# Two transformer blocks on one core: order of the last residuals, sums of squares and gate products as split matmuls

## The reference

```python
def rmsnorm(x, g):
    return x * rsqrt(mean(x * x, -1) + EPS) * g

def second_block(x, ...):                       # x: output of the first block
    proj = rmsnorm(x, norm1_g) @ w_in
    xa, ya, sq, sk, sv, dq, dk, dv = split(proj)
    xa = causal_dwconv(xa, conv_a_w) + conv_a_b              # 4 taps
    r = sigmoid(einsum('bsnc,ncd->bsnd', xa, w_rgate) + b_r) # 8 blocks of 64
    i = sigmoid(einsum('bsnc,ncd->bsnd', xa, w_igate) + b_i)
    a = exp(-8 * r * softplus(-lam))
    h = scan(a, sqrt(1 - a * a) * i * xa)       # the recurrence
    mixed = concat(h * gelu(ya), stick_breaking(sq, sk, sv), diff_attention(dq, dk, dv))
    x = x + mixed @ w_out
    u = causal_dwconv(rmsnorm(x, norm2_g) @ w_ff_up, conv_ff_w) + conv_ff_b
    x = x + (silu(u_gate) * u_val) @ w_ff_down
    return rmsnorm(x, final_g)
```

## Time and profile before

| | us |
|---|---|
| median of 3 runs | 1553.34 (1552.59 to 1553.67) |
| profiled execution | 1555.63 |
| its span in the trace | 1553.9 |
| PE busy | 1539.9 (99%) |
| DVE busy | 747.5 (48%) |
| ACT busy | 395.1 (25%) |
| POOL busy | 905.7 (58%) |
| mean granted clock of PE | 0.999 |

### The profile page before, as it was taken

How to read it: one execution, slowest core, us unless ns; L and a number is a source line. 1 busy time by engine, 2 the same in 40 slices (tenths; PEclk the granted TensorE clock), 3 DMA queues, 4 the chain that set the end, 5 groups by cost and what they waited for, 6 DMA issues and landing times.

```text
span 1553.9 us, 22779 instructions
## 1 busy us (share of the span) xinstructions
PE 1539.9 (99%) x7847; PEld 1291.7 (83%) x7847; DVE 747.5 (48%) x1157; ACT 395.1 (25%) x757; POOL 905.7 (58%) x536
## 2 busy tenths in 40 slices
PE   8999999999999999999999999999999999999998
PEld 7779999988888888888888888777877888888887
DVE  4157840232335354742343245868567751552456
ACT  4221210233442012210010013456564320220122
POOL 5645556544445667766666666653454666666653
PEclk9999999999999999999999999999999999999999
DMA  6223333322223432333333333322222323333322
GB/s 213 82 72 91 85 93 91 86 68 59 64 68 104 147 95 82 108 94 95 100 100 98 95 88 102 93 70 64 60 67 82 94 81 108 96 98 103 95 81 95
DMA packets 266712, 142.67 MB, mean 92 GB/s; under 512 B 6445, under 2 KB 263749, under 8 KB 266389
## 3 DMA queue, kind: packets, MB, share of 16 engines
q1 hardware_dynamic: 265285, 139.16, 30.5%
q10 hardware_dynamic: 1360, 2.56, 0.4%
HBM read 137.38 MB, written 4.19 MB: 91 GB/s over the span
## 4 chain that ended last, share of the span: by engine, by line
PE 95%; DVE 3%; ACT 1%; issue 1%; DMA 0%; ACTq 0%; DVEq 0%
PE PS L645 74%; PE PS L643 12%; PE PS L872 1%; PE PS L849 1%; PE PS L957 1%; PE PS L797 1%; DVE BL L2051 1%; PE PS L875 0%; PE PS L923 0%; PE PS L848 0%; PE PS L862 0%; DVE L L1881 0%; PE PS L1003 0%; DVE L L1864 0%; ACT SBX L1422 0%
## 5 line engine op out<-in xcount | busy, mean ns | idle before, releaser
L586 POOL TENSOR_TENSOR WL<-RAW,WH 128x1024 fp32r<-128x1024 f32 (+1 forms) x259 | 622.7, 2404 | 21.6
L584 POOL TENSOR_SCALAR WH<-RAW 128x1024 fp32r<-128x1024 f32 (+1 forms) x259 | 280.4, 1083 | 607.6 <-DMA RAW<-in_w_in_dram 257.5
L645 PE MATMUL PS<-BH,WH 128*128 128x512 f32 x928 | 366.6, 395 | 1.2 <-DVE BL L2051 1.1
L645 PE MATMUL PS<-BL,WH 128*128 128x512 f32 x928 | 361.4, 389 | 0.0
L645 PE MATMUL PS<-BH,WL 128*128 128x512 f32 x928 | 361.1, 389 | 0.0
L645 PEld LDWEIGHTS PS<-BH,WH 128*128 128x128 f32 x928 | 174.2, 188 | 42.4 <-issue 4.4
L645 PE MATMUL PS<-AH,WH 128*128 128x512 f32 x528 | 205.9, 390 | 0.0
L645 PE MATMUL PS<-AL,WH 128*128 128x512 f32 x528 | 205.4, 389 | 0.0
L645 PE MATMUL PS<-AH,WL 128*128 128x512 f32 x528 | 205.4, 389 | 0.0
L645 PEld LDWEIGHTS PS<-BH,WL 128*128 128x128 f32 x928 | 174.3, 188 | 37.2 <-issue 1.7
L645 PEld LDWEIGHTS PS<-BL,WH 128*128 128x128 f32 x928 | 174.2, 188 | 36.6
(11 more groups left out here) (334 smaller groups left out, 1817.4 us busy)
## 6 DMA issues: line engine op xcount, KB each, us to landing
RAW<-in_w_in_dram SPq DMA_DIRECT2D x89, 512.0 KB, 3.4
RAW<-in_w_ff_up_dram SPq DMA_DIRECT2D x44, 512.0 KB, 3.6
RAW<-in_w_gate_dram SPq DMA_DIRECT2D x22, 512.0 KB, 3.6
RAW<-in_w_up_dram SPq DMA_DIRECT2D x22, 512.0 KB, 3.6
RAW<-in_w_down_dram SPq DMA_DIRECT2D x16, 512.0 KB, 3.6
RAW<-in_w_ff_down_dram SPq DMA_DIRECT2D x16, 512.0 KB, 3.6
RAW<-in_w_out_dram SPq DMA_DIRECT2D x10, 512.0 KB, 3.7
RAW<-in_w_conv_out_dram SPq DMA_DIRECT2D x8, 512.0 KB, 3.7
```

The lines of the kernel that those rows point to most:

```text
L584: nc.gpsimd.tensor_scalar(WH[:, slot, 0:kc], RAW[:, slot, 0:kc], 1.0, 1.0, ALU.mult, ALU.mult).then_inc(w_hi, 1)
L586: nc.gpsimd.tensor_tensor(WL[:, slot, 0:kc], RAW[:, slot, 0:kc], WH[:, slot, 0:kc].bitcast(F32), ALU.subtract).then_inc(w_ready, 1)
L645: last = mm(bank_of(name, i)[0:rows], w[:, w_at, k, 0:rows], a[:, k, :], start=st, stop=sp_)
```

## The change

Three edits.

1. `last_residual` 0 to 3 come ahead of `BL` 0, and residual o + 4 behind `BL` o.
2. The sums of squares are made from parts: ACT copies `SS` to `SSH`, DVE subtracts to `SSL`, PE multiplies `ONE` (a float32r copy of `ones`) with both; the same for `SSB` at n1. `ONE` is written twice, as its place is used for other tiles in between.
3. The gate products are made from parts: `WRH`/`WRL` once, ahead of the residuals of dn2, and `XCH` (ACT, `xc_high`) and `XCL` (DVE, `xc_low`) for each group; three matmuls for each product. DVE's order in the recurrence is new as the diff shows: the reciprocal of `RF` moves behind decay 1.

```diff
@@ -196,6 +196,10 @@
         YA = place(rq2, "YA", [P, 4, T])
+        rq4 = again(r_q, q0 + 8448)
+        SSH = place(rq4, "SSH", [P, T], F32R)
+        SSBH = place(rq4, "SSBH", [P, T], F32R)
+        ONE = place(rq4, "ONE", [P, P], F32R)
         L = [place(again(r_q, q0), "L0", [P, 2, 2, T]), place(again(r_b, b0 + 4 * 8 * T), "L1", [P, 2, 2, T])]
@@ -210,6 +214,9 @@
         DQK = place(rx3, "DQK", [P, 4, T])
+        rx4 = again(r_x, x0)
+        WRH = place(rx4, "WRH", [P, 2, 4, P], F32R)
+        WRL = place(rx4, "WRL", [P, 2, 4, P], F32R)
@@ -229,6 +236,9 @@
         HG = place(again(r_g, g0), "HG", [P, KC, T])
+        rg4 = again(r_g, g0)
+        XCH = place(rg4, "XCH", [P, 4, T], F32R)
+        XCL = place(rg4, "XCL", [P, 4, T], F32R)
@@ -260,9 +270,11 @@
         SQB = place(rt9, "SQB", [P, 2, T])
+        SSBL = place(again(rt9, rt9[0]), "SSBL", [P, T], F32R)
         SSB = place(rt9, "SSB", [P, T])
...
         SQT = place(rt4, "SQT", [P, 2, T])
+        SSL = place(again(rt4, rt4[0]), "SSL", [P, T], F32R)
         SS = place(rt4, "SS", [P, T])
@@ -347,6 +359,8 @@
         ss_added = {n: sem(f"ss_added_{n}") for n in LATE}
+        SUM_USE = {"ffn": 0, "n1": 1, "n2": 3}
+        ss_hi, ss_lo, one_ready = sem("ss_hi"), sem("ss_lo"), sem("one_ready")
         ss_summed = {n: sem(f"ss_summed_{n}") for n in LATE}
@@ -713,8 +728,10 @@
-                pe.wait_ge(ss_added[name], KC + 2)
-                mm(PX[:, 0, 0:T], ones[:], SS[:], start=True, stop=True).then_inc(ss_summed[name], 1)
+                pe.wait_ge(one_ready, 2 if name == "n2" else 1)
+                pe.wait_ge(ss_lo, SUM_USE[name] + 1)
+                mm(PX[:, 0, 0:T], ONE[:], SSH[:], start=True, stop=False)
+                mm(PX[:, 0, 0:T], ONE[:], SSL[:], start=False, stop=True).then_inc(ss_summed[name], 1)
@@ -907,20 +924,24 @@
-                pe.wait_ge(ss_added["n1"], KC + 2)
-                mm(PX[:, 0, 0:T], ones[:], SS[:], start=True, stop=True)
-                mm(PX[:, 1, 0:T], ones[:], SSB[:], start=True, stop=True).then_inc(ss_summed["n1"], 1)
+                pe.wait_ge(ss_lo, SUM_USE["n1"] + 2)
+                for n, (own, after_b) in enumerate(((SSH, SSBH), (SSL, SSBL))):
+                    mm(PX[:, 0, 0:T], ONE[:], own[:], start=n == 0, stop=n == 1)
+                    last = mm(PX[:, 1, 0:T], ONE[:], after_b[:], start=n == 0, stop=n == 1)
+                last.then_inc(ss_summed["n1"], 1)
             stage("xa", b_t, n1, late=1, then=between_sums)
-            pe.wait_ge(small_loaded, 16 * (6 + 4))
+            pe.wait_ge(wr_lo, 1)
             pe.wait_ge(rt_ready["n1"], 2)
...
                 panel("dqk", c, c, b_t, n1)
-                pe.wait_ge(xc_ready, c + 1)
+                pe.wait_ge(xc_lo, c + 1)
                 if c >= 1:
...
                 for g in range(2):
-                    mm(RGATE[g], WR[:, g, c, :], XC[:, c, :], start=True, stop=True).then_inc(rg_done, 1)
+                    for n, (w, a) in enumerate(((WRH, XCH), (WRL, XCH), (WRH, XCL))):
+                        last = mm(RGATE[g], w[:, g, c, :], a[:, c, :], start=n == 0, stop=n == 2)
+                    last.then_inc(rg_done, 1)
@@ -1328,6 +1349,8 @@
             def root(name):
+                act.wait_ge(ss_added[name], KC + 2)
+                go(SSH[:], SS[:], ACT.Copy).then_inc(ss_hi, 1)
                 act.wait_ge(ss_summed[name], 1)
@@ -1344,6 +1367,8 @@
+            act.wait_ge(small_loaded, 16 * (6 + 4))
+            go(WRH[:], WR[:], ACT.Copy).then_inc(wr_hi, 1)
             with act.Fori(0, KC // 2) as i:
@@ -1354,6 +1379,9 @@
                     go(SQB[:, j], pick(H, c), ACT.Square, scale=VEC[:, 0, bass.ds(c + V_FIN, 1)]).then_inc(sq_ready["n1"], 1)
+            act.wait_ge(ss_added["n1"], KC + 2)
+            go(SSH[:], SS[:], ACT.Copy).then_inc(ss_hi, 1)
+            go(SSBH[:], SSB[:], ACT.Copy).then_inc(ss_hi, 1)
             act.wait_ge(fin_ms, 1)
@@ -1385,7 +1413,13 @@
+            def xc_high(c):
+                act.wait_ge(xc_ready, c + 1)
+                go(XCH[:, c], XC[:, c], ACT.Copy).then_inc(xc_hi, 1)
+
             for c in range(4):
+                if c == 2:
+                    xc_high(0)
                 act.wait_ge(freed["dve"], LETGO["xa"]["dve"] + c + 1)
@@ -1408,7 +1442,10 @@
+            go(small[:, 35:36], eps_t[:], ACT.Tanh)
             for c in range(4):
+                if c < 3:
+                    xc_high(c + 1)
                 decays(c)
@@ -1738,6 +1775,7 @@
             nc.vector.memset(WR[:], 0.0).then_inc(wr_cleared, 1)
+            ts(ONE[:], ones[:], 1.0, None, ALU.mult).then_inc(one_ready, 1)
             step(nc.vector.memset(XA[:, :, 0:3], 0.0))
@@ -1784,7 +1822,12 @@
+            def sum_low(name, whole, hi, lo, n=1):
+                dve.wait_ge(ss_hi, SUM_USE[name] + n)
+                tt(lo[:], whole[:], hi[:].bitcast(F32), ALU.subtract).then_inc(ss_lo, 1)
+
             def late_scale(name):
+                sum_low(name, SS, SSH, SSL)
                 dve.wait_ge(rt_ready[name], 1)
@@ -1815,6 +1858,8 @@
+            dve.wait_ge(wr_hi, 1)
+            tt(WRL[:], WR[:], WRH[:].bitcast(F32), ALU.subtract).then_inc(wr_lo, 1)
             dve.wait_ge(a_lo, A_USE["act2"] + GROUPS[2][1])
@@ -1833,6 +1878,8 @@
+            sum_low("n1", SS, SSH, SSL)
+            sum_low("n1", SSB, SSBH, SSBL, 2)
             dve.wait_ge(ss_summed["n1"], 1)
@@ -1893,6 +1940,10 @@
+            def xc_low(c):
+                dve.wait_ge(xc_hi, c + 1)
+                tt(XCL[:, c], XC[:, c], XCH[:, c].bitcast(F32), ALU.subtract).then_inc(xc_lo, 1)
+
             def gelu_inner(h):
@@ -1937,16 +1988,20 @@
             scaled("xa", 3, XA[:, 3, 3:T + 3])
+            xc_low(0)
             conv_a(1)
             scaled("dqk", 0, DQK[:, 0])
+            xc_low(1)
             conv_a(2)
+            scaled("dqk", 1, DQK[:, 1])
+            xc_low(2)
+            conv_a(3)
+            decay(0)
+            xc_low(3)
+            scaled("dqk", 2, DQK[:, 2])
+            decay(1)
             dve.wait_ge(rt_ready["n1"], 2)
             step(nc.vector.reciprocal(RF[:], RF[:]))
-            scaled("dqk", 1, DQK[:, 1])
-            conv_a(3)
-            decay(0)
-            scaled("dqk", 2, DQK[:, 2])
-            decay(1)
             decay(2)
@@ -2044,14 +2100,14 @@
-            for o in range(2):
+            for o in range(4):
                 last_residual(o)
...
                     op0=ALU.mult, op1=ALU.subtract).then_inc(b_lo, 1)
-                for r in ((2, 3, 4), (5,), (6,), (7,))[o] if o < 4 else ():
-                    last_residual(r)
+                if o < 4:
+                    last_residual(o + 4)
             dve.sem_inc(ss_added["n2"], 3)
```

More of the change, by code:

```diff
@@ L369, in two_blocks @@
         act_step, dve_step = sem("act_step"), sem("dve_step")
+        wr_hi, wr_lo, xc_hi, xc_lo = sem("wr_hi"), sem("wr_lo"), sem("xc_hi"), sem("xc_lo")
         cl_ready, lam_e = sem("cl_ready"), sem("lam_e")
```

## The result

The changed kernel takes **1559.52 us** (median of 6 runs, 1557.11 to 1560.15) against 1553.3 (6 runs, 1552.59 to 1553.68) of the kernel before: ratio **1.0037 [1.0027, 1.0047]**. Forecast was 1553.8 with a range up to 1556.3: wrong, and slower by more than a measurement's uncertainty.

A forecast was written before the change was run, and what follows sets the result against it. PE, busy 99% of the span, was taken as the bound. ffn -0.44, n1 -0.3, recurrence +1.0 and n2 +0.25 gave +0.5 on the median 1553.34: 1553.8 us, range 1549.9 to 1556.3.

The forecast's parts named there:

- Matmuls in parts: Sums at ffn, n1, n2 and gate products: split matmuls replace plain ones, cutting PE's work by 3.35 us.
- Rival D: Gate products: a split one is no cheaper, 1.6 lost and 3.5 added, 1558.9 us; chance 0.02.
- A: Whole kernel: the waits don't form and the full saving is seen, -5.4, 1547.9 us; chance 0.12 (or most of it).
- B: Half the saving: short dqk 3 wait (0.7), subtraction at n2 escapes POOL; -1.6, 1551.7 us; chance 0.19.
- n1: Sums at n1: of 0.86 us saved, 0.3 is left, as PE waits 0.45 and restarts 0.1 late.
- `WRL` hidden: Ahead of the residuals of dn2: making the weights' parts (about 1.1 us) falls in DVE's idle 2.02 and costs nothing.
- dqk 3 late for the second dv panel: End of the recurrence: dqk 3 is scaled only at 1029.4, behind `RF` and decay 2, so PE waits 2.4 us.
- Rival C: Recurrence: DVE becomes the bound, PE waits 1.1 at each of the last three gate products; +3.3, 1557.1 us; chance 0.12.
- PE waits 2.4, from 1027.0 to 1029.4: Second dv panel: PE idles 2.4 us for dqk 3, turning the recurrence's 1.6 gain into a loss of 1.0.
- PE waits 2.4, and its sum ends at 1197.6: Sum of n2: PE idles 2.4 us for the subtraction that meets POOL's pass; the sum ended at 1197.36 before.
- comes out 0.25 slower: Stretch n2: residual order, low parts and split sum together, with its 0.44 saving included, lose 0.25 us.
- ffn: Sum at the norm ffn: the split matmul saves 0.44 us; copy and subtraction are covered and cost nothing.

The follow-up runs named there:

- e1_fill_both: Changed kernel with 18 transposes of a constant ahead of the second dv panel and 18 ahead of the sum of n2: 1556.48 us, ratio 1.0018.
- b0_before: The kernel before, unchanged, run and profiled again: 1553.33 us, ratio 1.0000; its profiled execution took 1552.63.
- e5_resid_only: Kernel before with only the new order of residuals and low parts: 1554.71 us, ratio 1.0008.
- e7_old_order: Changed kernel with the old order of residuals and low parts: 1553.96 us, ratio 1.0006.
- e0_after: The changed kernel as it is, run and profiled again: 1559.3 us, ratio 1.0035; its profiled execution took 1560.59.
- e2_rf_late: Changed kernel with the reciprocal of `RF` moved from behind decay 1 to behind the differential attention: 1555.73 us, ratio 1.0010.
- e3_plain_n2: Changed kernel with the sum of squares of n2 as one plain float32 matmul again, without copy and subtraction: 1555.69 us, ratio 1.0016.
- e8_best: Changed kernel with the old order of residuals and low parts and the reciprocal of `RF` behind the differential attention: 1551.11 us, ratio 0.9987.
- e6_late_sum: Changed kernel with the reciprocal of `RF` behind the differential attention and the sum of n2 behind the whole panel 2 of gv0: 1551.59 us, ratio 0.9990.

## Why the prediction was wrong, step by step

**Matmuls in parts: right.** The six gate matmuls start at the pitch of split ones (PE's timeline after, first turn and second):

```profile
999.14 0.50 PE L943 MATMUL PS<-XCH,WRH 128*128 128x512 f32 x1
...
1000.65 0.39 PE L660 MATMUL PS<-BH,WH 128*128 128x512 f32 x1
...
1006.12 0.39 PE L943 MATMUL PS<-XCH,WRH 128*128 128x512 f32 x1
...
1007.50 0.39 PE L660 MATMUL PS<-BH,WH 128*128 128x512 f32 x1
```

The two gate products of a turn without a wait take 1.38 (1006.12 to 1007.50) against 1.76 before: 0.38 saved of 0.40 forecast. The first turn waits 0.28 for its low part and has slow starts after it, and saves nothing; together 1.1, where 1.6 less 0.2 was forecast. Rival D is out, and so are A and B, which need the waits at dv and n2 to be short or absent.

**n1: right.** An idle time of 0.28, and a start 0.44 behind the due one (forecast 0.45); from PE's due start at 981.01 to the second matmul behind the sums at 982.72 it is 1.71, before 1.95: 0.24 saved, forecast 0.3.

```profile
980.78 0.39 PE L660 MATMUL PS<-BL,WH 128*128 128x512 f32 x1
981.45 0.50 PE L929 MATMUL PS<-SSH,ONE 128*128 128x512 f32 x1 [0.28 <-DVE SSBL L1827]
...
982.72 0.40 PE L660 MATMUL PS<-BH,WL 128*128 128x512 f32 x1
```

**`WRL` hidden: right, barely.** It took 1.64 where I had 1.1, and DVE's idle time ahead of the first residual shrank from 2.02 to 0.43.

```profile
941.67 1.64 DVE L1862 TENSOR_TENSOR WRL<-WR,WRH 128x1024 fp32r<-128x1024 f32 x1
...
945.00 0.69 DVE L1871 SCALAR_TENSOR_TENSOR H<-PS,H 128x512 f32<-128x512 f32 x1 [0.43 <-PE PS L660]
```

**dqk 3 late for the second dv panel: right in place and size.** DVE's queue (the row of 2.48 is decay 2, held by POOL's pass):

```profile
1022.17 3.34 DVE L2004 RECIPROCAL RF<-RF 128x512 f32<-128x512 f32 x1
1025.43 2.48 DVE L1956 SCALAR_TENSOR_TENSOR TH<-A,TH 128x512 f32<-128x512 f32 x1
...
1028.44 0.68 DVE L1894 TENSOR_TENSOR DQK<-PS,R 128x512 f32<-128x512 f32 x1
```

The walk down to it was close all along: low parts 1, 2 and 3 were done at 1004.9, 1011.8 and 1018.8, where 1005.5, 1012.1 and 1019.1 were forecast. dqk 3 is ready at 1029.1 and PE restarts at 1029.22 (forecast 1029.4) after 2.40 (forecast 2.4). Rival C, waits of 1.1 at three gate products, didn't come.

**First failed step: "PE waits 2.4, from 1027.0 to 1029.4", and likewise "PE waits 2.4, and its sum ends at 1197.6".** Each wait was priced at its own length. On the chip a wait of this kind is followed, in part of the executions, by 3.4 us at 1.2 GHz, 1.5 to 1.6 dearer. e1_fill_both, which leaves the lateness and takes only the idle time, puts this term at 2.8 of the changed kernel's median, between one fall and two; the prediction had it at nothing. The profile in front couldn't show it for these places, as it had no wait of such a length in a dense stretch; a bound for it was owed.

**Second failed step: the stretch n2 "comes out 0.25 slower", carried over to the median.** The walk itself was good (0.4 by the profile in front). Its base was not: "0.8 lost, since residual 2 waits behind `BL` 0" and "1.8 lost to late low parts" are properties of an execution that took 1555.63, 2.3 above the median. I noted the 2.3 and then added the difference to the median as if the waits stood in the median too. Two waits worth 2.6 inside an execution that is 2.3 too long should have been tied together: the gain of taking them away can't be had from executions that don't have them. Against the 25.56 of b0_before the changed stretch is 28.55: **+3.0 instead of +0.25**. e5_resid_only and e7_old_order share it out: the new order alone +1.3; the split sum alone -0.4; both together +3.0, since the order brings the end of the additions 3.2 later (25.7 behind the start of wo2b instead of 22.5) and the split adds its copy and subtraction to just that path.

**The sum again**, between the changed kernel's profile and b0_before's: ffn -0.4, n1 -0.2, gate products -1.1, dv wait with its restart +2.5, one clock fall +1.5, n2 +3.0: +5.3; the spans differ by 5.2. The second execution of the changed kernel adds another fall (1.6), 0.4 in its wait at the start (5.1 and 5.5), and small waits. In the medians, the forecast +0.5 with the 2.8 of the first failed step and the 2.75 of the second (3.0 less 0.25) makes +6.05; measured were +6.2 and, in e0_after, +5.9.

**Left open.** Why a wait of 2.2 to 2.5 brings a fall in one execution and none in the next. Seven such waits were profiled, and four of them had a fall behind: both of e0_after and the one of e2_rf_late, the dv wait of the changed kernel's first profile but not its n2 wait of 2.42, and neither the 2.2 of e3_plain_n2 nor that of e7_old_order. Length doesn't sort them, as a wait of 2.42 had no fall and one of 2.39 had. Nor was an execution like e8_best's one of 1556.1 traced; whether it has the cause of the few long ones of the kernel before isn't known.

## What to carry to other kernels

A profile is one execution: set its own time against the median first, and if it lies well above, look for the waits that make up that excess and give no edit the credit for removing them. Price a new idle time of the matmul engine in dense work, of the 2.2 to 2.5 us seen here, at its length plus, in part of the executions, a stretch at half clock; here, moving the operation that waits a half panel later was worth 4.1 (e6_late_sum against e2_rf_late), where splitting it saves 0.44 of work. Before putting short operations ahead of one that shares a lock with another engine, check on which side of that engine's long instruction it is now issued: 0.3 us of order was worth 2 us of that operation's time.

## What the runs showed of the hardware that was not expected

A single idle time of 2.4 us in a TensorE stream that is otherwise dense was enough for the granted clock to drop to 0.50, and it did so not during the idle time but 1.0 to 1.5 us after work had resumed (in the four falls that were profiled; 1029.22 to 1030.66 and 1200.13 to 1201.13 are two). It stayed there for 3.4 us although PE was busy throughout. With 2.13 us of each idle time filled by 128x128 transposes the one trace shows no fall, and all 11 runs have a mean clock of 0.999 or 1.0.

Of 13 profiled executions nine have `BL` 0 caught by POOL's subtraction (1.98 to 2.97) and four have it free (0.75 or 0.76). In these four it started 0.1 to 0.3 ahead of that instruction, while POOL's copy still ran, and POOL's subtraction took 2.72 to 2.89 for 2.40; in the profile in front it started 0.06 after the copy's end, and lost.
